# Layer 0's modulation in two parts: 8 slabs in the setup, 16 beside the query and key tiles

## What is computed

```
m = silu(cond) @ ada_w[i] + ada_b[i]          # 1024 x 6144, for c_ctx and for c
sh_m, sc_m, g_m, sh_f, sc_f, g_f = split(m, 6)
x = x + g_m * mixer(rms_norm(x) * (1 + sc_m) + sh_m)
x = x + g_f * mlp(rms_norm(x) * (1 + sc_f) + sh_f)
```

## Time and profile before

| | |
|---|---|
| median of three runs (lowest, highest) | 2887.68 us (2887.18, 2888.81) |
| profiled execution, its time | 2887.49 us |
| profiled execution, its span of instructions | 2885.3 us |
| TensorE busy, mean granted clock | 2581.8 us (89%), 0.935 of 2.4 GHz |
| VectorE, ScalarE, GpSimd busy | 1138.5, 869.6, 350.3 us |
| modulation matmuls (L266), all layers | 1536 records, 120.5 us |
| query and key tiles (L803), three layers | 672 records, 231.0 us |

### The profile page before, as it was taken

One profiled execution on the slowest core, in us unless ns is written; L12 is line 12 of the kernel. 1 busy time (PEld: TensorE's weight loads), 2 busy tenths in 40 slices (PEclk: granted clock), 3 DMA queues, 4 the chain that ended last, 5 costly groups with the idle time before them and its releaser, 6 DMA issues. The chain is left out here.

```text
span 2885.3 us, 50959 instructions
## 1 busy us (share of the span) xinstructions
PE 2581.8 (89%) x21484; PEld 2075.4 (72%) x21484; DVE 1138.5 (39%) x2121; ACT 869.6 (30%) x1580; POOL 350.3 (12%) x339
## 2 busy tenths in 40 slices
PE   5798889997998887888899999678999999889999
PEld 2356569996667776776599985445999966548999
DVE  1233543334314555543333333452333322625443
ACT  1133433333113333231233232331333322533332
POOL 0000020110013334331111100001111100002111
PEclk7799989998999999999899999758999999998999
DMA  8722046664220000000366642002666522113331
GB/s 274 230 88 73 28 155 197 204 199 118 73 88 21 11 7 7 7 7 5 117 204 198 194 157 82 19 0 88 199 193 193 176 98 82 50 59 116 118 130 66
DMA packets 310241, 312.66 MB, mean 108 GB/s; under 512 B 14306, under 2 KB 308012, under 8 KB 309932
## 3 DMA queue, kind: packets, MB, share of 16 engines
q1 hardware_dynamic: 302784, 304.08, 32.9%
q10 hardware_dynamic: 7276, 5.95, 0.7%
HBM read 305.55 MB, written 4.46 MB: 107 GB/s over the span
## 5 line engine op out<-in xcount | busy, mean ns | idle before, releaser
L586 PE MATMUL psum<-parts 128*128 128x384 f32 x6144 | 1117.8, 340 | 42.3 <-POOL parts L668 42.3
L586 PEld LDWEIGHTS psum<-parts 128*128 128x128 f32 x6144 | 1074.5, 190 | 89.4 <-issue 45.0
L682 DVE TENSOR_TENSOR parts<-slab,parts 128x2048 fp32r<-128x2048 f32 x128 | 293.5, 2293 | 207.1 <-ACT parts L628 207.1
L628 ACT ACTIVATE parts<-slab 128x2048 fp32r<-128x2048 f32 x128 | 244.2, 1908 | 374.1 <-PE psum L586 368.8
L382 DVE SCALAR_TENSOR_TENSOR xT<-psum,mod,xT 128x128 f32<-128x128 f32 x320 | 118.2, 413 | 445.4 <-PE psum L586 281.0
L803 PE MATMUL psum<-hT,slab 128*128 128x384 f32 x672 | 231.0, 499 | 13.6 <-DVE hT L364 13.5
L674 POOL TENSOR_TENSOR parts<-room_mlp,parts 128x384 fp32r<-128x384 f32 x128 | 130.2, 1018 | 878.4 <-DVE room_mlp L692 878.4
L803 PEld LDWEIGHTS psum<-hT,slab 128*128 128x128 f32 x672 | 130.7, 195 | 100.4 <-issue 18.3
L668 POOL TENSOR_TENSOR parts<-hT,parts 128x384 fp32r<-128x384 f32 x32 | 31.9, 1003 | 1126.9 <-ACT parts L659 1126.9
L692 DVE TENSOR_TENSOR room_mlp<-hT 128x384 f32<-128x384 f32 x128 | 71.4, 558 | 246.6 <-ACT hT L633 246.6
L633 ACT ACTIVATE hT<-psum 128x384 f32<-128x384 f32 x128 | 62.9, 491 | 328.0 <-PE psum L586 328.0
(11 more groups left out here) (237 smaller groups left out, 3118.8 us busy)
## 6 DMA issues: line engine op xcount, KB each, us to landing
slab<-in_mlp_w SPq DMA_DIRECT2D x128, 1024.0 KB, 5.3
ada_slab<-in_ada_w SPq DMA_DIRECT2D x96, 1024.0 KB, 7.5
slab<-in_da_wqkv SPq DMA_DIRECT2D x24, 1024.0 KB, 5.1
slab<-in_rwkv_wrkv SPq DMA_DIRECT2D x12, 1024.0 KB, 5.2
slab<-in_da_wo SPq DMA_DIRECT2D x8, 1024.0 KB, 5.1
slab<-in_swa_wqkv SPq DMA_DIRECT2D x6, 1024.0 KB, 5.0
slab<-in_rwkv_wo SPq DMA_DIRECT2D x4, 1024.0 KB, 5.1
slab<-in_swa_wo SPq DMA_DIRECT2D x4, 1024.0 KB, 5.3
```

What stands on the lines that cost most here:

```text
L586: mm = nc.tensor.matmul(out, x(a), y(b), start=first and n == 0, stop=last and n == 2)
L628: nc.scalar.activation(w[:, r % 2, 0], slab[:, g % SLOTS], ACT.Copy).then_inc(sem("hi_ready"), 1)
L682: nc.vector.tensor_tensor(w[:, r % 2, 1], slab[:, (start + r) % SLOTS], w[:, r % 2, 0].bitcast(F32), ALU.subtract).then_inc(split_ready, 1)
```

## The change

Layer 0's modulation is cut into three groups of eight slabs. The setup takes the first group, which is shift and scale of the mixer, and adds 1 to that scale alone; the norm of layer 0's attention waits for this one. The other 16 slabs are taken in the attention's block: one slab's products behind each of the 16 query and key tiles on TensorE, a group's copy on ScalarE at the head of steps 8 and 16, its turn on TensorE at the end of those steps, its bias on VectorE at step 10 and behind the last step, with the second scale. TensorE waits for the last bias before it transposes the keys. On SP, two modulation slabs stand before each of weight slabs 4 to 11. The strip and the turn's constant are widened for eight slabs, with the working room 40 numbers smaller. (In `qk_act` and `qk_dve` the call of `beside` stands at the head of a step.)

```diff
+        FIRST_GROUP = 8
+        FIRST_GROUPS = ADA_UNITS // FIRST_GROUP
         STRIP = 32
-        CONDAT = 2 * (ADA_GROUP - 1)
+        CONDAT = 2 * (FIRST_GROUP - 1)
...
+        def ada_group(layer, it):
+            return FIRST_GROUPS + (layer - 1) * ADA_GROUPS + it
+        def first_load(sp, u):
+            if u >= ADA_SLOTS:
+                sp.wait_ge(sem("ada_free"), u + 1 - ADA_SLOTS)
+            sp.dma_start(ada_slab[:, u % ADA_SLOTS], cols(I["ada_w"][0], u * SLAB)).then_inc(sem(f"ada_ready{u % ADA_SLOTS}"), 16)
+        def first_unit(pe, u):
+            s = u % FIRST_GROUP
+            pe.wait_ge(sem(f"ada_ready{u % ADA_SLOTS}"), 16 * (u // ADA_SLOTS + 1))
+            if s == 0 and u:
+                pe.wait_ge(sem("rows_ready"), u // FIRST_GROUP)
+            for k in range(KT):
+                strip = STRIP * (k % 4)
+                mm = nc.tensor.matmul(psum[strip:strip + STRIP, 6, 0:SLAB], cond_pad[:, k, CONDAT - 2 * s:CONDAT - 2 * s + STRIP],
+                                      ada_slab[:, u % ADA_SLOTS, k], start=s == 0 and k < 4,
+                                      stop=s == FIRST_GROUP - 1 and k >= 4)
+            mm.then_inc(sem("ada_free"), 1)
+        def first_turn(pe, it, rows, b):
+            pe.wait_ge(sem("rows_ready"), it + 1)
+            if it:
+                pe.wait_ge(sem("mod_step"), it)
+            for h in range(2):
+                mm = nc.tensor.matmul(psum[:, b, 2 * FIRST_GROUP * h:2 * FIRST_GROUP * (h + 1)], rows[:, h * P:(h + 1) * P],
+                                      K["add_parts"], start=True, stop=True)
+            mm.then_inc(sem("rows_turned"), 1)
+        def first_rows(act, it, rows):
+            act.wait_ge(sem("ada_free"), FIRST_GROUP * (it + 1))
+            if it:
+                act.wait_ge(sem("rows_turned"), it)
+            nc.scalar.activation(rows, psum[:, 6, 0:SLAB], ACT.Copy).then_inc(sem("rows_ready"), 1)
+        def first_take(dve, it, b):
+            dve.wait_ge(sem("rows_turned"), it + 1)
+            n = 2 * FIRST_GROUP
+            dst = mod[:, 0, it * n:(it + 1) * n, :].rearrange("p (s h) g -> p h s g", h=2)
+            bias = ada_b[:, it * n:(it + 1) * n].rearrange("p (s h) -> p h s", h=2)
+            for h in range(2):
+                ins = nc.vector.tensor_tensor(dst[:, h], psum[:, b, n * h:n * (h + 1)].rearrange("p (s g) -> p s g", g=2),
+                                              bias[:, h].unsqueeze(2).to_broadcast([P, FIRST_GROUP, 2]), ALU.add)
+            ins.then_inc(sem("mod_step"), 1)
+        def first_scale(dve, c):
+            m = mod[:, 0, c * KT:(c + 1) * KT, :]
+            nc.vector.tensor_scalar(m, m, 1.0, None, ALU.add).then_inc(sem("mod_ready"), 1)
...
-                dve.wait_ge(sem("mod_ready"), 2 * (layer + 1))
+                dve.wait_ge(sem("mod_ready"), 1 if layer == half == 0 else 2 * (layer + 1))
...
-                    for s in range(ADA_GROUP):
-                        ada_load(sp, 0, 0, s)
-                    with sp.Fori(1, ADA_GROUPS) as it:
-                        for s in range(ADA_GROUP):
-                            ada_load(sp, 0, it, s)
+                    for u in range(FIRST_GROUP):
+                        first_load(sp, u)
...
-                    def group(it):
-                        for s in range(ADA_GROUP):
-                            ada_unit(pe, 0, it, s)
-                        ada_turn(pe, 0, it, mod_rows)
-                    group(0)
-                    with pe.Fori(1, ADA_GROUPS) as it:
-                        group(it)
+                    for u in range(FIRST_GROUP):
+                        first_unit(pe, u)
+                    first_turn(pe, 0, mod_rows, 2)
...
-                    with dve.Fori(0, ADA_GROUPS) as it:
-                        ada_take(dve, 0, it)
-                    ada_scale(dve, 0)
+                    first_take(dve, 0, 2)
+                    dve.wait_ge(sem("mod_step"), 1)
+                    first_scale(dve, 1)
...
+                if beside:
+                    beside(pe, n)
...
+            more = layer == 0
+            mod_rows = c(SLAB)
+            def pe_beside(pe, n):
+                u = FIRST_GROUP + n
+                if u < ADA_UNITS:
+                    first_unit(pe, u)
+                if n and n % FIRST_GROUP == 0:
+                    first_turn(pe, n // FIRST_GROUP, mod_rows, 7)
+            def act_beside(act, n):
+                if n and n % FIRST_GROUP == 0:
+                    first_rows(act, n // FIRST_GROUP, mod_rows)
+            def dve_beside(dve, n):
+                if n == FIRST_GROUP + 2:
+                    first_take(dve, 1, 7)
             with nc.Block() as block:
                 @block.sync
                 def _(sp):
-                    load_phase(sp, name, f"wo{layer}")
+                    if more:
+                        for u in range(SLOTS, phases[name][1]):
+                            for a in range(2 * (u - SLOTS), 2 * (u - SLOTS) + 2):
+                                if FIRST_GROUP + a < ADA_UNITS:
+                                    first_load(sp, FIRST_GROUP + a)
+                            load_unit(sp, name, u)
+                        load_first(sp, f"wo{layer}")
...
-                    qk_pe(pe, start, n_tiles, dst, ws)
+                    qk_pe(pe, start, n_tiles, dst, ws, pe_beside if more else None)
                     v_pe(pe, start, v_units, n_tiles)
+                    if more:
+                        pe.wait_ge(sem("mod_step"), FIRST_GROUPS)
...
+                    qk_dve(dve, link, n_tiles, dst, gain, ws, dve_beside if more else None)
+                    if more:
+                        first_take(dve, 2, 7)
+                        dve.wait_ge(sem("mod_step"), FIRST_GROUPS)
+                        first_scale(dve, 4)
```

More of the change, by code:

```diff
@@ L100, in constants @@
     c[:, CONST_COLS["ident64"]] = r == s
-    c[:, CONST_COLS["add_parts"]] = p % 32 == q[:, :12]
+    c[:, CONST_COLS["add_parts"]] = p % 32 == q[:, :16]
     c[:, CONST_COLS["restart"]] = (np.arange(TOK) % CH != 0)[None, :]
@@ L145, in build @@
         lam = sb("lam", 8)
-        ROOM = 27744
+        ROOM = 27704
         psum = ctx.enter_context(nc.psum_tensor("psum", [P, 8, 512], F32))
@@ L290, in ada_turn @@
         def ada_turn(pe, layer, it, rows):
-            g = layer * ADA_GROUPS + it
+            g = ada_group(layer, it)
             pe.wait_ge(sem("rows_ready"), g + 1)
@@ L294, in ada_turn @@
             for h in range(2):
-                mm = nc.tensor.matmul(mod_cols(h), rows[:, h * P:(h + 1) * P], K["add_parts"], start=True, stop=True)
+                mm = nc.tensor.matmul(mod_cols(h), rows[:, h * P:(h + 1) * P],
+                                      K["add_parts"][:, 0:2 * ADA_GROUP], start=True, stop=True)
             mm.then_inc(sem("rows_turned"), 1)
         def ada_take(dve, layer, it):
-            g = layer * ADA_GROUPS + it
+            g = ada_group(layer, it)
             dve.wait_ge(sem("rows_turned"), g + 1)
@@ L309, in ada_scale @@
         def ada_scale(dve, layer):
-            dve.wait_ge(sem("mod_step"), (layer + 1) * ADA_GROUPS)
+            dve.wait_ge(sem("mod_step"), ada_group(layer, ADA_GROUPS))
             for c in (1, 4):
@@ L450, in _ @@
                             .then_inc(sem("lam_exps"), 1)
-                    with act.Fori(0, ADA_GROUPS) as it:
-                        ada_rows(act, 0, it, mod_rows)
+                    first_rows(act, 0, mod_rows)
                 @block.gpsimd
@@ L787, in wo_dve, with qk_pe @@
                 residual(layer, 0, g, bank(banks[g % len(banks)], TOK)).then_inc(acc_taken, 1)
-        def qk_pe(pe, start, n_tiles, dst, ws):
+        def qk_pe(pe, start, n_tiles, dst, ws, beside=None):
             for n in range(n_tiles + 2):
@@ L817, in qk_pe, with qk_act @@
                         .then_inc(sem("partner"), 1)
-        def qk_act(act, start, n_tiles, ws):
+                if beside:
+                    beside(pe, n)
+        def qk_act(act, start, n_tiles, ws, beside=None):
             runs, hb = run_after[start - 1] if start else 0, base("head_sq")
             for n in range(n_tiles + 1):
+                if beside:
+                    beside(act, n)
                 if n < n_tiles:
@@ L838, in qk_act, with qk_dve @@
                         .then_inc(sem("head_std"), 1)
-        def qk_dve(dve, link, n_tiles, dst, gain, ws):
+        def qk_dve(dve, link, n_tiles, dst, gain, ws, beside=None):
             hb = base("head_sq")
             for n in range(n_tiles + 1):
+                if beside:
+                    beside(dve, n)
                 if n < n_tiles:
@@ L929, in _ @@
                 def _(sp):
-                    load_phase(sp, name, f"wo{layer}")
+                    if more:
[5 more added lines that the diff above has]
+                        load_first(sp, f"wo{layer}")
+                    else:
+                        load_phase(sp, name, f"wo{layer}")
```

(5 more changed lines are left out.)

2 lines of the change are left out of this document (1 added, 1 removed).

## The result

| | before | after |
|---|---|---|
| median of the timed runs, us | 2887.43 (2883.41 to 2888.81, 4 runs) | 2857.75 (2855.91 to 2861.53, 4 runs) |
| profiled execution, us | 2887.49 | 2855.91 |
| its span, us | 2885.3 | 2853.8 |
| mean granted clock | 0.935 | 0.949 |
| first tile / first product of values, us | 108.73 / 213.78 | 60.12 / 186.78 |

After over before is 0.9901, 95% interval 0.9884 to 0.9918: 29.7 us, against a forecast of 30.8.

A forecast was written before the change was run, and what follows sets the result against it. It took modulation-slab transfers to bound the setup and TensorE the query and key tiles. -48.3 - 0.1 + 15.0 + 0.4 + 1.2 + 1.0 = -30.8 us gave 2856.7 us, range 2853 to 2866.

The forecast's parts named there:

- Removed: Setup: the first norm waits for slab 7 instead of slab 23, first tile near 60.3 us; 48.3 and 0.1 us out.
- Added on TensorE: Query and key tiles: fifteen slabs' products on the path at 1.00 us each, 15.0 us (14.0 to 16.1).
- the drain: Tiles: switching between strips and whole array twice per slab drains TensorE; 1.1 us in sum, already in the slab price.
- Wait at slab 8: Behind tile 0: slab 8's load queues behind query weights and cache loads; TensorE waits 1.2 us (0 to 3.0).
- Waits at the even slabs: Behind every second tile, slabs 10 to 22: loads issued late on SP's queue; about 1.0 us together (0 to 2.5).
- above 1 us at the even slabs: Sign against the forecast: TensorE waits this long for even slabs among the tiles, where under 0.7 was expected.
- The turns and the tail: First turn behind tile 8 costs 0.4 us; slab 23 and second turn fit gaps behind tile 15: 0, at most 1.5.
- From there on every stage is as long as before: From the products of values, begun near 183 us, to the end: no stage changes length.
- late slabs: Rival, tiles: three loads in a row lengthen waits, 1.5 us at seven places, 3 at slab 8; 2870 us; 14 in 100.
- The clock did not fall: Rival "Slower": waits at every second tile take TensorE to 1.2 GHz, up to 116 us more, 2973; 3 in 100.
- The transfers did not set the pace of the tiles: Rival "No gain": DMA engines, not TensorE, pace the tiles, so nothing is won, 2887 us; 2 in 100.

The follow-up runs named there:

- the run without waits: The changed kernel with loads of slabs 8 to 23 cut to an eighth of each, all instructions and waits kept; 2855.86 us.

## Why the prediction was right, and where it was not

- **Removed.** The last setup slab at 51.94 and the first tile at 60.12, for 52.07 and 60.3: 48.6 us for 48.4. Slab 8's landing was worked out as 69.4 from the two transfer rates of the earlier trace rows; its products started at 69.39.
- **Added on TensorE: mis-sized.** 15 x 1.19 = 17.9 us for 15.0, above the upper end of 16.1 as well. The step that failed is the reading of the earlier trace rows. It took the price from the start of the slab to the start of what follows (1.00), which leaves out the delay ahead of the slab and the one that shows only in the following matmuls. The period tells it. In layer 3's MLP no slab stands between the same products: 216 us hold 1248 records at clock 1.00, so 48 take 8.31 us. In layer 0's MLP 48 records and a slab take 572.74 - 563.22 = 9.52. So a slab cost 1.21 in the MLP already, nearly the 1.19 among the tiles, and these rows of the kernel before were there to be read (the second with its columns as in the earlier trace rows):

```profile
572.74 1.07 PE L266 MATMUL psum<-ada_slab,cond_pad 128*32 128x256 f32 x16
```

```profile
2660.00:2876.00 216.00, 216.00 (x1248) 216.00 (x1247) 89.59 (x105) 71.07 (x73) 24.41 (x24) 1.00 0.32 103
```

  The prediction weighed the drain, too, and found 0.07 per slab, 1.00 less 0.93. The 0.93 was a third of a row's length, whose end is modelled; from start to start three slabs take 2.62 (32.75 to 35.37 in the run with five more places), 0.87 each. The runs show 0.32 to 0.33 where the prediction had 0.07.
- **Wait at slab 8.** 1.52 us of idle time for 1.2, right in kind; tile 0 ended a little earlier than the earlier trace rows moved. The loss against the run without waits is 1.59 (60.12 to 69.39 against 59.97 to 67.65).
- **Waits at the even slabs.** The sum was 1.0 us and came to 1.4 (0.30 at slab 10, 1.14 at slab 16, each the partner-to-slab time over 0.53), but not as described. Slab 10 waited as forecast, at the lower end of 0.3 to 0.7. At the five others without a fetch nothing waited: the margin was forecast at -0.1 to 0.3, and the beat was 0.19 longer than reckoned. The one long wait, at slab 16, has a cause that the prediction didn't have, the instruction fetch, and it broke the prediction's own line of "above 1 us at the even slabs".
- **The turns and the tail.** 0.47 for 0.4 (130.89 to 131.36), and 0.14 for the 0 taken.
- **The sum.** To the values -48.6 + 17.9 + 1.6 + 1.4 + 0.5 + 0.1 = -27.1, measured 186.78 - 213.78 = -27.0. The forecast was -30.8, so 3.8 us were missed, 2.9 of them in the price of a slab. The profiled run nevertheless came out 31.6 us shorter, because from the values on it was 4.5 us faster (2663.0 for 2667.5). "From there on every stage is as long as before" was therefore wrong in this execution; on average over four traces it is 2.6 us. The total was right to 0.8 us by two misses of opposite sign. What the change does, where, and its order of size are shown; that the two misses cancel, 3 to 4 us each, was luck, and the cause of the second is open.
- **Rivals.** No late slabs as a rule (one in seven, from another cause). The clock did not fall: TensorE waited 1.52 us for a transfer at slab 8 and 1.08 at slab 16 and kept 1.00. The page TensorE: Matmul & The Clock Gate of the Trainium skill, section HAM oscillation — how this bites in real kernels, tells of bursts of matmuls that are shorter than the DMA wait behind them, and start cold every time. One wait of that kind stands in the setup, 4.47 us behind three slabs of 2.80 together, and from there on it runs at 0.50; the waits among the tiles are shorter than the work between them, of 7 us and more. The transfers did not set the pace of the tiles either: the DMA share there was 0.66, and with small loads the beat stayed at 7.44.

## What to carry to other kernels

Take the price of an inserted operation from the period of the pattern with it, less the period without it, not from its start to the start of the next. Work that a first use does not need can move from a stage full of transfers into one full of matmuls; what it then costs is its TensorE time and the changes of tiling, and setting two such pieces together pays for the changes once (here 0.32 us less a pair). Before work is moved out of a transfer-bound stage, look for stretches in which the DMA engines stand still: here five more places gave another 13 us up to the values.

## What the runs showed of the hardware

- A group of matmuls in strips of 32 columns, set among 128x128 ones, cost 0.33 us over its own pace at 2.4 GHz (1.19 for 0.86): 0.10 ahead of it, 0.10 in the matmuls that follow, 0.13 between its first product and the next tile. Two slabs side by side paid it once, and slabs over the whole array had neither of the 0.10.
- One fetch of 16 KB of instructions holds one of 16 DMA engines for about 1.1 us and can delay the landing of a 1 MB load by as much (9.1 us for 7.9, at slab 16 and, with the fetch moved, at slab 14); four other fetches of the changed kernel's trace delayed none.
- 64 matmul records of 8 columns took 13.8 us in the setup, 0.22 us each at 1.2 GHz, and the loading of weights was busy for 13.69 of 13.70 us there: where each matmul loads its own weights, few columns did not make it cheap.
- In a stage where TensorE is busy for about 70% of the time, the same code ran at a mean clock of 0.53 in one execution and 0.73 in another.
